# Low parts of weights one unit later, stick-breaking in smaller steps, and another order at the recurrence's end

## The reference

```python
z = jnp.einsum('bhqd,bhkd->bhqk', qb, k[:, :, :end])
mask = jnp.arange(end)[None, :] < qpos[:, None]
u = jnp.where(mask, jax.nn.softplus(z), 0.0)
a = jnp.where(mask, jnp.exp(z - _rev_cumsum(u)), 0.0)
o = jnp.einsum('bhqk,bhkd->bhqd', a, v[:, :, :end])
```

## Time and profile before

| | us |
|---|---|
| median of 3 runs | 3816.99 |
| lowest and highest of them | 3814.59, 3817.51 |
| the profiled execution | 3824.99 |
| its span (first to last instruction) | 3823.3 |

### The profile page before, as it was taken

The page is one execution under the profiler, slowest core; times in us unless marked ns, Lnnn a source line. Parts: engine busy times, 40 slices in busy tenths (PEclk is TensorE's granted clock), DMA queues, the critical chain, the costliest instruction groups (busy, mean ns, idle before and its releaser), DMA issues.

```text
span 3823.3 us, 53603 instructions
## 1 busy us (share of the span) xinstructions
PE 3664.8 (96%) x23179; PEld 2984.5 (78%) x23179; DVE 1795.9 (47%) x2449; ACT 1324.7 (35%) x2053; POOL 295.4 (8%) x328
## 2 busy tenths in 40 slices
PE   7999999999999999999999899998999999599998
PEld 6777888877788878888887778886877767488887
DVE  4434434455543455443444344335666756455443
ACT  4444322344432332332334432224343332343222
POOL 1011100100110111110100011011000000000001
PEclk9999999999999999999999999998999999799999
DMA  6212323321233232323231132323221221332332
GB/s 207 73 51 77 98 86 103 100 67 60 90 95 103 86 99 90 98 94 104 89 93 56 46 98 88 105 91 94 68 78 52 73 59 60 129 116 84 106 97 66
DMA packets 333375, 337.71 MB, mean 88 GB/s; under 512 B 11873, under 2 KB 323795, under 8 KB 332628
## 3 DMA queue, kind: packets, MB, share of 16 engines
q1 hardware_dynamic: 332722, 334.16, 28.0%
q10 hardware_dynamic: 418, 0.12, 0.0%
HBM read 319.55 MB, written 14.68 MB: 87 GB/s over the span
## 4 chain that ended last, share of the span: by engine, by line
PE 89%; ACT 4%; DVE 4%; issue 2%; DMA 1%; ACTq 0%; POOL 0%; SPq 0%; POOLq 0%; DVEq 0%
PE P L99 88%; ACT sA L114 2%; ACT hi L113 1%; PE P L102 1%; DVE lo L117 1%; DVE x L117 0%; DVE rw_S L117 0%; DMA scr<-held_dram 0%; ACTq L157 0%; ACT scr L114 0%; DMA vg<-held_v_dram 0%; DVE rw_r L125 0%; DMA rows<-in_shift_b_dram 0%; ACT aH L113 0%; DVE aL L125 0%
## 5 line engine op out<-in xcount | busy, mean ns | idle before, releaser
L117 DVE TENSOR_TENSOR lo<-raw,hi 128x1024 fp32r<-128x1024 f32 (+2 forms) x617 | 738.8, 1198 | 1177.4 <-ACT hi L113 1176.2
L99 PE MATMUL P<-aH,lo 128*128 128x512 f32 x2840 | 1139.3, 401 | 24.4 <-DVE q L125 7.2
L99 PE MATMUL P<-aH,hi 128*128 128x512 f32 x2840 | 1112.5, 392 | 0.0
L99 PE MATMUL P<-aL,hi 128*128 128x512 f32 x2840 | 1112.3, 392 | 0.0
L113 ACT ACTIVATE hi<-raw 128x1024 fp32r<-128x1024 f32 (+2 forms) x617 | 610.8, 991 | 1008.4 <-PE P L99 1002.3
L99 PEld LDWEIGHTS P<-aH,lo 128*128 128x128 f32 x2840 | 536.8, 189 | 156.6 <-issue 23.1
L99 PEld LDWEIGHTS P<-aH,hi 128*128 128x128 f32 x2840 | 536.4, 189 | 114.1
L99 PEld LDWEIGHTS P<-aL,hi 128*128 128x128 f32 x2840 | 537.3, 189 | 110.4 <-issue 4.7
L99 PE MATMUL P<-bH,lo 128*128 128x512 f32 x1088 | 426.6, 392 | 16.3 <-DVE bL L117 16.3
L99 PE MATMUL P<-bL,hi 128*128 128x512 f32 x1088 | 425.3, 391 | 0.0
L99 PE MATMUL P<-bH,hi 128*128 128x512 f32 x1088 | 425.1, 391 | 0.0
(11 more groups left out here) (292 smaller groups left out, 3846.5 us busy)
## 6 DMA issues: line engine op xcount, KB each, us to landing
raw<-in_w_ffn_in_dram SPq DMA_DIRECT2D x176, 512.0 KB, 3.6
raw<-in_w_in_dram SPq DMA_DIRECT2D x163, 512.0 KB, 3.6
raw<-in_w_ffn_out_dram SPq DMA_DIRECT2D x96, 384.0 KB, 3.1
raw<-in_w_ffn_dram SPq DMA_DIRECT2D x36, 512.0 KB, 3.6
raw<-in_w_o_dram SPq DMA_DIRECT2D x26, 512.0 KB, 3.5
raw<-in_w_ffn_dram SPq DMA_DIRECT2D x32, 384.0 KB, 3.1
raw<-in_w_mem_kv_dram SPq DMA_DIRECT2D x16, 512.0 KB, 4.3
raw<-in_w_ffn_out_dram SPq DMA_DIRECT2D x16, 512.0 KB, 3.5
```

The costliest lines, as they stand in the source:

```text
L99: return self.e.matmul(out, l, r, start=start, stop=stop, skip_group_check=skip) if self.e else Nothing()
L117: return self.e.tensor_tensor(out, a, b, op) if self.e else Nothing()
```

## The change

**Weights.** `split` falls into `split_high(unit + 3)`, which is ScalarE's part, and `split_low(unit + 2)`, which is VectorE's and at which SyncE issues its fetch. Fewer units lie between a fetch and its use: three instead of four.

**Stick-breaking.** `stick_log`, `stick_plus`, `stick_high` and `stick_low` are steps of one bank (`FLAT[n]`) each, with costs for ScalarE, VectorE and GpSimd apart, and `arrange` keeps a queue of each engine. No instruction is added; the places between other instructions are new.

**End of the recurrence.** The last 12 steps of the held projections wait, in the planner, for the sixth pair's end. `rw_store` comes ahead of GELU; `vg` is loaded in four DMAs; the reload of `x` comes last. Centring is merged with the affine part: `sgu_norm(q, j)` is two SCALAR_TENSOR_TENSOR of 128 x 512 for each half j of each of four position tiles q, in place of one TENSOR_SCALAR and two TENSOR_TENSOR of 128 x 1024 a tile. `sgu_inverse` does Ln and Exp for all four tiles at once. `sgu_mix(g)` waits for the halves g // 4 only. `wsn`, `wsT`, `bs` and `hold1` lie elsewhere in SBUF.

```diff
-    def __init__(self, name, *args, pe=0.0, lat=0.0, far=3.0, dve=0.0, wait=0.15, gap=0.1, hold=False, needs=(), gives=(),
-                 group=None, last=False):
+    def __init__(self, name, *args, pe=0.0, lat=0.0, far=3.0, act=0.0, dve=0.0, pool=0.0, wait=0.15, gap=0.1, hold=False, needs=(),
+                 gives=(), group=None, last=False):
...
-        if s.dve:
-            v = max(v, end + s.wait) + s.dve
+        if any(s.parts):
+            v = end + s.wait
+            for i, took in enumerate(s.parts):
+                if took:
+                    v = free[i] = max(v, free[i]) + took
...
-        out += [Step("stick_scores", l, h, u, pe=2.2, lat=7.0, needs=[("qkv", l, h // 2)], far=0.0, gives=[("scored", l, h)]),
-                Step("stick_split", l, h, u, lat=3.5), Step("stick_sums", l, h, u, pe=2.5, lat=4.0),
...
+        out += [Step("stick_scores", l, h, u, pe=2.2, far=0.0, needs=[("qkv", l, h // 2)] + ([("head", l, h - 2)] if h > 1 else []),
+                     gives=[("scored", l, h)])]
+        for b in range(3):
+            out += [Step("stick_log", l, h, u, b, far=0.0, act=(1.9, 1.9, 1.25)[b], gives=[("ln", l, h, b)])]
...
-    side = [Step("load_v", needs=[("end", 6)], lat=1.0)]
-    side += [Step("rw_store", p, lat=0.8, needs=[("end", p)], gives=[("o", 6)] if p == 6 else []) for p in range(7)]
-    side += [Step("sgu_stats", q, lat=3.0) for q in range(4)]
...
+    side = [Step("load_v", needs=[("end", 6)])]
+    side += [Step("rw_store", p, far=0.0, dve=0.62, wait=0.7, hold=p == 7, needs=[("end", p)], gives=[("o", p)]) for p in range(8)]
+    side += [Step("sgu_load"), Step("first_u", needs=[("held",)]), Step("load_gates"), Step("load_x_back")]
+    side += [Step("sgu_gelu", q, lat=3.0 if q == 0 else 1.0) for q in range(4)] + [Step("first_gates")]
+    side += [Step("sgu_stats", q, dve=1.5, hold=True) for q in range(4)] + [Step("sgu_inverse", lat=7.0), Step("sgu_turn", pe=0.9, dve=1.4, hold=True)]
+    side += [Step("sgu_norm", q, 0, dve=1.55, hold=True) for q in range(4)]
+    side += [Step("sgu_norm", q, 1, far=0.0, dve=1.55, gives=[("ln", q)]) for q in range(4)]
...
+    held = jobs_steps(held_jobs(), 1)
+    for s in held[len(held) - 12:]:
+        s.needs += (("end", 6),)
...
-                order.append(("split", unit[key] + AHEAD))
+                order += [("split_high", unit[key] + AHEAD), ("split_low", unit[key] + AHEAD - 1)]
...
-        e.wait_ge(*S.evict.at(("ln", 3)))
+        e.wait_ge(*S.evict.at(("ln", 3, g // 4)))
...
-        e.tt(y, y, m["lnw"][:, :], ALU.mult).then_inc(*S.evict.up())
+        e.stt(y, y, ag[:, 0:1], m["lnw"][:, n], ALU.subtract, ALU.mult).then_inc(*S.evict.up())
+        e.wait_ge(*S.act_turn.at("ln"))
         e.wait_ge(*S.evict.now())
-        e.tt(y, y, m["lnb"][:, :], ALU.add).then_inc(*S.evict.up(("ln", q)))
+        e.stt(y, y, rs, m["lnb"][:, n], ALU.mult, ALU.add).then_inc(*S.evict.up(("ln", q, j)))
```

More of the change, by code:

```diff
@@ L207, in job_steps @@
                                     needs=job.needs if cg == job.c0 and pi == 0 else job.later if pi else (),
-                                    lat=job.lat if end else 0.0, dve=job.dve * tiles if end else 1.25 if mi == 0 and ka == 0 else 0.0,
+                                    lat=job.lat if end else 0.0, act=tiles / 2 * 1.75 if end and job.form == "N" else 1.05 if mi == 0 and ka == 0 and grain > 1 else 0.0,
+                                    dve=1.25 if mi == 0 and ka == 0 and not end else job.dve * tiles if end and job.form == "T" else 0.0,
                                     gives=job.gives if end and cg + job.width >= job.c0 + job.ncols else ()))
@@ L266, in stick_steps @@
     for h in heads:
-        out += [Step("stick_scores", l, h, u, pe=2.2, lat=7.0, needs=[("qkv", l, h // 2)], far=0.0, gives=[("scored", l, h)]),
-                Step("stick_split", l, h, u, lat=3.5), Step("stick_sums", l, h, u, pe=2.5, lat=4.0),
-                Step("stick_values", l, h, u, pe=2.2, lat=1.0, far=7.0, needs=[("mem", l)] if h >= 4 else [], gives=[("head", l, h)])]
+        out += [Step("stick_scores", l, h, u, pe=2.2, far=0.0, needs=[("qkv", l, h // 2)] + ([("head", l, h - 2)] if h > 1 else []),
+                     gives=[("scored", l, h)])]
+        for b in range(3):
+            out += [Step("stick_log", l, h, u, b, far=0.0, act=(1.9, 1.9, 1.25)[b], gives=[("ln", l, h, b)])]
+        for b in range(3):
+            out += [Step("stick_plus", l, h, u, b, far=0.0, wait=0.0, dve=(0.7, 0.7, 0.42)[b], pool=(0.3, 0.55, 0.3)[b], needs=[("ln", l, h, b)],
+                         gives=[("log", l, h, b)])]
+        for b in range(3):
+            out += [Step("stick_high", l, h, u, b, far=0.0, wait=0.0, act=(0.6, 0.6, 0.35)[b], needs=[("log", l, h, b)], gives=[("high", l, h, b)])]
+        for b in range(3):
+            out += [Step("stick_low", l, h, u, b, far=0.0, wait=0.0, dve=(0.69, 0.69, 0.42)[b], needs=[("high", l, h, b)],
+                         gives=[("split", l, h, b)])]
+        out += [Step("stick_sums", l, h, u, pe=2.6, far=0.0, act=1.4, pool=1.0, needs=[("split", l, h, b) for b in range(3)],
+                     gives=[("exp", l, h)]),
+                Step("stick_values", l, h, u, pe=2.2, far=0.0, act=0.6, dve=0.69, needs=[("exp", l, h)] + ([("mem", l)] if h >= 4 else []),
+                     gives=[("head", l, h)])]
     return out
@@ L2080, in fetch, with split_low @@
                   ).then_inc(*S.weights_in[s].up(u, by=16))
-    def split(u):
-        fetch(u + NSLOT)
+    def split_low(u):
+        if u > 2:
+            fetch(u + NSLOT)
     def load_mem():
@@ L2153, in load_v @@
             e.wait_ge(*S.held_out[i % 2].at(i))
-        e.dma(m["vg"][:, :, :], d["held_v"]).then_inc(*S.v_in.up(0, by=16))
+        for q in range(4):
+            e.dma(m["vg"][:, q, :], d["held_v"][:, q, :]).then_inc(*S.v_in[q].up(0, by=16))
     def load_u(g):
@@ L2187, in sgu_load, with first_u, load_gates, load_x_back @@
         e.dma(m["sb"][0:1, :], d["sgu_b_2"].rearrange("a g i -> a (g i)")).then_inc(*S.sgu_in.up(0, by=16))
-    def rw_store(p):
-        if p == 7:
-            for k in range(KT):
-                e.wait_ge(*S.operand_lo.at(("rw", "s", k)))
-            e.dma(m["x"][:, :, :], d["spill"].rearrange("p (k n) -> p k n", n=S_)).then_inc(*S.x_back.up(0, by=16))
+    def first_u():
+        load_u(0)
+        load_u(1)
+    def load_gates():
+        for i in range(4):
+            load_gate(i)
+    def load_x_back():
+        for k in range(KT):
+            e.wait_ge(*S.operand_lo.at(("rw", "s", k)))
+        e.dma(m["x"][:, :, :], d["spill"].rearrange("p (k n) -> p k n", n=S_)).then_inc(*S.x_back.up(0, by=16))
     def finish():
```

154 lines of the change are left out of this document (75 added, 79 removed).

## The result

| | median | runs | ratio to before, 95% interval |
|---|---|---|---|
| before | 3817.25 us | 4 (3814.59 to 3818.05) | |
| changed | 3727.52 us | 4 (3724.81 to 3730.51) | 0.9766 (0.9749 to 0.9783) |

The change saves 89.7 us. The forecast was 3745 us, 72 us faster, in a range of 3725 to 3772.

A forecast was written before the change was run, and what follows sets the result against it. TensorE was taken as the bound, busy 3664.8 of 3823.3 us, with gain only from its 158 us of standing and half-clock stretches. 38 + 26 + 8 = 72 us off 3817.0 gave 3745 us, range 3725 to 3772.

The forecast's parts named there:

- End of the recurrence, 38 us: Recurrence's end: 51.4 us of gaps and half clock, less 9.0 new gaps, 2 clock, 2 in the recurrence; bounds 20 and 50.
- New gaps: TensorE's remaining waits at the recurrence's end: 2.1 before proj_b, 2.3 eviction, 3.1 norm, 1.5 mixes' operands, together 9.0 us.
- Half clock: At the first mixes: a 3.1 us gap, near the 3.4 after which the clock fell, charged 2 us.
- Stick-breaking, 26 us: Layers 0 and 3: pieces shorten waits at x, q and mp, gain 13 us a layer; bounds 0 to 39.
- low parts, 8 us: Weights' low parts one unit later: 3.5 us at rw_KR, 4.5 at the other waits for x; bounds 0 and 12.
- rival 1: Stick-breaking gives little: pieces stand in ScalarE's queue, late sH or sL holds TensorE; gain 52, 3765 us, chance 0.16.
- residual of 6.6 us a layer: Stick-breaking, of 19.6 us a layer stays: 0.3 at mp, 1 at q, 2 at x, 2 at stick_sums, 1.3 clock.
- The later fetch, nothing: Weight loads get three units instead of four; landing takes 3.6 us, so hidden except perhaps at the start; charged 0.
- The table load: ScalarE, between first mixes' copies and next GELU of hold: one 1.28 us load beside hold's reload, charged nothing.
- Rival 3: More than forecast: residual gaps everywhere are half of those forecast, 3732 us, chance 0.08.
- Rival 2: Mixes' chain lies open: norm wait 6 us, half clock 5.8, recurrence loses 9; gain 58, 3759 us, chance 0.14.
- Rivals 1, 4 and 5: Besides rival 1: late fetches, 3868 us, chance 0.03; list changes but same semaphores come last, about 3810 us, chance 0.03.

The follow-up runs named there:

- only_end: The kernel before with only the other order at the recurrence's end (side, held, GELU, DMAs, sgu_norm): 3783.70 us, ratio 0.9906.
- fetch_late: The kernel before with only SyncE's weight fetches issued one unit later, low parts at their old place: 3817.01 us, ratio 1.0005.
- no_weights: The changed kernel with low parts of weights back at the old place, three units ahead, the other two parts kept: 3771.17 us, ratio 0.9873.
- norms_early: The changed kernel with Ln and Exp, sgu_turn and all sgu_norm halves placed between proj_b's steps, mixes still together: 3719.97 us, ratio 0.9743.
- mixes_apart: As norms_early, with the eight mixes placed one by one among products of proj_b's last two and proj_a's first two units: 3707.91 us, ratio 0.9717.

## Why the prediction was right, and where it was not

**The direction and the bound.** Right: the whole gain is waits and half-clock work. TensorE's gaps over 0.4 us went from 140.5 to 64.5 us in total (counted behind its first instruction), and its busy time fell by 17.1 us where I forecast about 18. But the number was saved by the width of the range: 3727.5 lies 2.5 us inside its lower end and outside the forecast's own 3733 to 3757. Of the signs that I named, all came but one: the half-clock stretches at the end, forecast under 5 us together, are 30.7 us.

**End of the recurrence, 38 us.** Alone it measured 36 us (`only_end`, 30 to 42 by its interval), so the size is right. Its terms are not. New gaps: 9.0 forecast, 1.9 + 2.2 + 0.7 = 4.9 measured (unrounded). The wait for the norm was 2.2 us and the eviction's 2.3 did not come on top of it. It came later and smaller: the 0.7 us are the third mix waiting for the eviction of the first, which VectorE reaches only behind the second halves of all four tiles. VectorE's last pass and that eviction, then TensorE:

```profile
3246.93 0.75 DVE L125 SCALAR_TENSOR_TENSOR vg<-vg,st,lnb 128x512 f32<-128x512 f32 x1
3247.60 0.68 DVE L117 TENSOR_TENSOR acc<-P,hold 128x512 f32<-128x512 f32 x1
```

```profile
3248.34 2.07 PE L99 MATMUL P<-sb,c 1*128 1x512 f32 x2 [0.70 <-DVE acc L117]
```

For the operands of the mixes, charged with 1.5 us, TensorE did not wait. Half clock: 2 forecast, 15 measured. The step that failed is "a gap of 3.1 us is near the one of 3.4 after which the clock fell: I charge 2 us": it looked at the gap and not at what TensorE does behind it, eight mixes in a row. The recurrence: 2 us of new gaps forecast; in the profiles it got 7.4 us shorter beyond the 10.9 that left, of which some 6 us belong to the one execution of before that was profiled (604.8 us against 598.6 in `fetch_late`), and the 1 us left is too small to read. I also gave the change of ScalarE's order and of SyncE's queue causes that the runs don't bear out: one of the order and the cover would have done most at `bL`, and the place of the reload of `x` is worth nothing with `proj_b` in between.

**Stick-breaking, 26 us, and low parts, 8 us.** This step failed by its split. Alone, the pieces with the planner's queues are worth 21 and the low parts 37 us, and the pieces leave the wait at `x` at 6.3 us without the low parts. I had read that `lo` stood ahead of `q`, `x` and `mp` and then priced the low parts only at `rw_KR` and the other waits for `x`; rival 1 even argued that the low part only came last because it stood behind the chain. It came last since ScalarE's `hi` stood behind the same chain. The residual of 6.6 us a layer was also too much: no gap over 0.4 us is left in layers 0 and 3. The first block gained 52.7 us by the profiles where I had 26 and part of the 8. The wait for `rw_KR` is gone as forecast; it is there with 3.5 us in `no_weights`.

**The later fetch, nothing.** Right (`fetch_late`), also at the start: its first block ends within 1 us of that of the kernel before.

**The table load.** ScalarE in the changed kernel between the first mixes and the next GELU:

```profile
3249.57 1.28 ACT L114 ACT_TABLE_LOAD   x1
3251.03 0.63 ACT L114 ACTIVATE hold<-hold 128x512 f32<-128x512 f32 x1 [0.19 <-DMA hold<-held_dram]
```

The load takes 1.28 us and `hold` begins 0.19 us after that for the DMA, not for a drain: on the path it costs nothing, as charged. The figure of 2.66 us that the Trainium skill gives ("ScalarE: Activation LUTs", section "What ACT_TABLE_LOAD costs") is not seen here either.

**The rivals.** Rival 3 (the residual gaps are half of mine, 3732 us) came nearest in number and in part in kind: 4.9 of 9.0 us of gaps were left at the end, and of 6.6 us a layer in stick-breaking next to nothing; it had no word on the low parts' place or the clock. Rival 2 was right in one of its three parts, the clock at the mixes, with 15 us where it had 5.8; what it named in its favour, eight mixes in a row, is what `norms_early` and `mixes_apart` bear out. Its other two parts did not come (2.2 us for the norm, not 6, and no loss in the recurrence). Rivals 1, 4 and 5 did not come. The error in the end's clock (13 us too little) and that in the first block (some 22 us too little gain) went against each other; that the total is better than its terms is luck.

## What to carry to other kernels

Where a chain of engines prepares an operand (load, high part, low part), let the low part stand a unit later in the common order than the high part that it waits for; otherwise it waits in its queue for an engine that is itself waiting, and holds every eviction behind it. Two units were worse here than one. Such a margin gives its full gain at a place only if the wait that comes next in the same queue is taken away too: measure such edits together and apart, and by stage, since here the total did not show it. It is worth a run to spread small products (one row, or 128 columns) among large ones, even with no gap around them: here eight groups in a row brought TensorE's clock to half, and placing the normalizations early and the groups apart gave 17 to 20 us.

## What the runs showed of the hardware

TensorE's granted clock fell from 1.00 to 0.50 while the profile has the engine busy without a gap (17.00 of 17.00 us in `norms_early`), in a row of one-row and 128-column products, and came back to 1.00 during the 512-column products that followed; with the same products spread out it stayed at 1.00 (`mixes_apart`). Not expected was also how little the time depends on the DMA side: moving a 2048 KB reload ahead of ten smaller loads (0.9765 against 0.9766), or every weight fetch one unit later (1.0005, 0.9996 to 1.0015), left it the same within the intervals.
